# A two-layer hybrid model kernel: four buffers for modulation weights, small inputs packed, and output projections opened on two column slabs at once

## What is computed

```python
c_act = jax.nn.silu(c)
for layer in range(DEPTH):                         # DEPTH = 2
    mod = c_act @ ada_w[layer] + ada_b[layer]      # 1024 -> 6144
    shift_m, scale_m, gate_m, shift_f, scale_f, gate_f = ...split(mod, 6)
    h = rmsnorm(x, norm_mix_g[layer]) * (1.0 + scale_m) + shift_m
    y = gdn_mixer(h, ...) if layer % 2 == 0 else mla_mixer(h, ...)
    x = x + gate_m * y
    h = rmsnorm(x, norm_ffn_g[layer]) * (1.0 + scale_f) + shift_f
    x = x + gate_f * swiglu(h, ffn_w_gate[layer], ffn_w_up[layer], ffn_w_down[layer])

def gdn_mixer(h, w_in, conv_w, a_log, dt_bias, norm_g, w_out):
    proj = h @ w_in                                # q, k, v, gate: 4 x 1024; a, b: 8 each
    qkv = silu(causal_depthwise_conv(qkv, conv_w)) # 4 taps
    beta, g = sigmoid(b_in), -exp(a_log) * softplus(a_in + dt_bias)
    o = chunk_gated_delta_rule(l2norm(q), l2norm(k), v, g, beta)   # per head, chunks of 64
    o = rmsnorm(o, norm_g) * silu(gate)
    return o @ w_out                               # 1024 x 1024
```

## Time and profile before

| | us |
|---|---|
| runs | 2572.89, 2578.45, 2578.01 |
| median | 2578.01 |
| the profiled execution | 2574.89 |
| its span in the profile | 2573.1 |

### The profile page before, as it was taken

One profiled execution on the slowest core, in us unless ns is written; L12 is line 12 of the kernel. 1 busy time (PEld: TensorE's weight loads), 2 busy tenths in 40 slices (PEclk: granted clock), 3 DMA queues, 4 the chain that ended last, 5 costly groups with the idle time before them and its releaser, 6 DMA issues.

```text
span 2573.1 us, 29814 instructions
## 1 busy us (share of the span) xinstructions
PE 2323.3 (90%) x12156; PEld 1831.7 (71%) x12156; DVE 1185.8 (46%) x1734; ACT 609.6 (24%) x1101; POOL 1204.3 (47%) x690
## 2 busy tenths in 40 slices
PE   4899998999999978889999997878898889989888
PEld 2677776778888755557888885556677767878766
DVE  5566666575454653225313136334452254554332
ACT  3243343131111232222202023332221121012112
POOL 1323222357777732115666665113446556656552
PEclk8999999899999989889999998889999999999989
DMA  6322222155555411002333332002223223323221
GB/s 212 98 86 67 80 76 65 57 165 172 189 164 191 136 64 35 25 25 77 104 98 94 96 93 80 25 25 67 72 73 92 81 82 107 97 83 98 83 82 58
DMA packets 361699, 236.23 MB, mean 92 GB/s; under 512 B 11126, under 2 KB 346204, under 8 KB 361436
## 3 DMA queue, kind: packets, MB, share of 16 engines
q1 hardware_dynamic: 360732, 230.40, 30.1%
q10 hardware_dynamic: 832, 3.93, 0.4%
HBM read 232.21 MB, written 2.10 MB: 91 GB/s over the span
## 4 chain that ended last, share of the span: by engine, by line
PE 82%; DVE 11%; ACT 3%; DMA 2%; issue 2%; POOL 1%; SPq 0%; DVEq 0%; ACTq 0%; POOLq 0%
PE bank L457 16%; PE bank L458 16%; PE bank L459 16%; PE bank L476 4%; PE bank L478 3%; PE bank L477 3%; PE bank L652 2%; PE bank L501 2%; DVE A L1774 2%; PE bank L971 1%; DMA WIDE<-in_ada_t 1%; PE bank L961 1%; DVE mx L1758 1%; PE bank L824 1%; PE bank L493 1%
## 5 line engine op out<-in xcount | busy, mean ns | idle before, releaser
L419 POOL TENSOR_SCALAR wH<-stage 128x1024 fp32r<-128x1024 f32 (+3 forms) x342 | 381.8, 1116 | 1312.7 <-PE bank L459 539.3
L421 POOL TENSOR_TENSOR wL<-stage,wH 128x1024 fp32r<-128x1024 f32 (+3 forms) x342 | 823.5, 2408 | 28.5
L457 PE MATMUL bank<-hH,wH 128*128 128x512 f32 x1108 | 439.9, 397 | 25.9 <-ACT A L1083 8.4
L458 PE MATMUL bank<-hL,wH 128*128 128x512 f32 x1108 | 435.8, 393 | 0.0
L459 PE MATMUL bank<-hH,wL 128*128 128x512 f32 x1108 | 435.3, 393 | 0.0
L457 PE MATMUL bank<-RA,wH 128*128 128x512 f32 (+1 forms) x900 | 327.5, 364 | 13.8 <-DVE A L1466 13.8
L458 PE MATMUL bank<-RA,wH 128*128 128x512 f32 (+1 forms) x900 | 325.8, 362 | 0.0
L459 PE MATMUL bank<-RA,wL 128*128 128x512 f32 (+1 forms) x900 | 325.8, 362 | 0.0
L457 PEld LDWEIGHTS bank<-hH,wH 128*128 128x128 f32 x1108 | 211.1, 191 | 76.1 <-issue 25.3
L459 PEld LDWEIGHTS bank<-hH,wL 128*128 128x128 f32 x1108 | 210.9, 190 | 44.6
L458 PEld LDWEIGHTS bank<-hL,wH 128*128 128x128 f32 x1108 | 211.2, 191 | 44.1 <-issue 0.7
(11 more groups left out here) (304 smaller groups left out, 3198.8 us busy)
## 6 DMA issues: line engine op xcount, KB each, us to landing
WIDE<-in_ada_t SPq DMA_DIRECT2D x48, 1024.0 KB, 5.9
stage<-in_ffn_w_gate SPq DMA_DIRECT2D x44, 512.0 KB, 3.8
stage<-in_ffn_w_up SPq DMA_DIRECT2D x44, 512.0 KB, 3.8
stage<-in_gdn_w_in SPq DMA_DIRECT2D x32, 512.0 KB, 4.1
stage<-in_ffn_w_down SPq DMA_DIRECT2D x32, 512.0 KB, 4.0
stage<-in_c_wkv SPq DMA_DIRECT2D x32, 512.0 KB, 3.8
stage<-in_o_w_in SPq DMA_DIRECT2D x32, 512.0 KB, 4.0
stage<-in_e_w_in SPq DMA_DIRECT2D x26, 512.0 KB, 3.8
```

Of the source, the lines that this page charges most:

```text
L419: pool.tensor_scalar(high[:, 0:n], raw[:, 0:n], 1.0, 0.0, ALU.mult, ALU.add).then_inc(w_high, 1)
L421: pool.tensor_tensor(low[:, 0:n], raw[:, 0:n], high[:, 0:n].bitcast(F32), ALU.subtract).then_inc(w_split, 1)
L457: pe.matmul(bank[:, 0:n], h[:, k, c], xh[:, k, :], start=first and k == 0, stop=False)
L458: pe.matmul(bank[:, 0:n], h[:, k, c], xl[:, k, :], start=False, stop=False)
```

## The change

**Start.** The first eight modulation groups use four slots (two of them in `A`), and a load waits for the sum four groups earlier. The small inputs are packed on the host: gate columns (`gdn_ab`, 128 x 128), three vectors of eight, the convolution rows behind the tables. SP's order is new: c first, group 0 ahead of x, and slabs 0 to 2 between groups 5, 6 and 7. The gate columns have weights of their own (`abH`, `abL`) and no place in the slab plan. PE makes gate columns, slab 0 and slab 1 together, chunk by chunk, as h comes. DVE's and ACT's work on the gates is moved between head 0's convolutions. The first five chunks of head 1 are done before head 0's squares and not at its start.

**Openings.** All 12 calls of `residual` run slabs 0 and 1 in step: chunk n of slab 0, chunk n of slab 1, chunk n+1 of slab 0.

**Last head.** Its fills now issue 14 chunk products (seven chunks of two slabs) of `gdn_out`, so that only chunk 7 is left for `residual`.

```diff
-PLAN = [("ab", 2), ("gdn", 32), ("gdn_out", 8)]
+PLAN = [("gdn", 32), ("gdn_out", 8)]
+ADA_SLOT = [n % 4 if n < ADA_HEAD else n % 2 for n in range(2 * ADA_LAYER)]
...
+        adaw = [t.rearrange(...) for t in (WIDE[:, 0:4], WIDE[:, 4:8], A[:, 8:12], A[:, 12:16])]
+        abH, abL = RA[:, 16, 0:2 * P], RA[:, 17, 0:2 * P]
...
             def load_ada(n):
-                if n >= 2:
-                    sp.wait_ge(ada_summed, n - 1)
+                if n >= 4:
+                    sp.wait_ge(ada_summed, n - 3 if n < ADA_HEAD else n - 1)
...
-            head_slabs(0)
+            for n in range(2, ADA_HEAD):
+                load_ada(n)
+                if n >= ADA_HEAD - 3:
+                    j = n - ADA_HEAD + 3
+                    load(SLAB0["gdn"] + j, vin[8 * j], KD)
+            load(SLAB0["gdn"] + 3, vin[24], KD)
...
+            def residual_chunk(name, xh, xl, kc, n, k, j):
+                s0, u0 = SLAB0[name], USE0[name]
+                if n == 0:
+                    pe.wait_ge(w_split, s0 + j + 1)
+                    free(j, u0 // 2)
+                h, l = (w[:, k, :] for w in halves(s0 + j, kc))
+                pe.matmul(acc[j][:], h, xh[:, k, :], start=n == 0, stop=False)
+                pe.matmul(acc[j][:], h, xl[:, k, :], start=False, stop=False)
+                mm = pe.matmul(acc[j][:], l, xh[:, k, :], start=False, stop=n == kc - 1)
+                if n == kc - 1:
+                    mm.then_inc(slab_done, 1)
...
+                for n in range(begun, kc):
+                    pe.wait_ge(ready, count - kc + n + 1)
                     for j in range(2):
+                        residual_chunk(name, xh, xl, kc, n, order[n] if order else n, j)
+                if behind:
+                    behind(0)
+                for i in range(2, KD):
+                    slab(s0 + i, i % 2, u0 // 2 + i // 2, xh, xl, kc)
...
-                def fill(*chunks):
+                def fill(first, end):
                     if ahead:
-                        head_sums(i + 1, range(*chunks))
+                        head_sums(i + 1, range(first, end))
+                    else:
+                        for c in range(14 * first // 32, 14 * end // 32):
+                            pe.wait_ge(y_ready, c // 2 + 1)
+                            residual_chunk("gdn_out", yH, yL, KD, c // 2, c // 2, c % 2)
-                fill(0, 5)
+                if i:
+                    fill(0, 5)
...
-            residual("gdn_out", yH, yL, KD, y_ready, 8, 1)
+            residual("gdn_out", yH, yL, KD, y_ready, 8, 1, begun=KD - 1)
```

More of the change, by code:

```diff
@@ L111 @@
     _s += _n
-    _u += {"ab": 0, "mla": 24}.get(_name, _n)
+    _u += 24 if _name == "mla" else _n
 NORM_OF = {"mix0": 0, "ffn0": 1, "mix1": 2, "ffn1": 3, "e": 4, "x0": 5, "o": 6, "x1": 7}
@@ L126 @@
 ADA_FFN = 20
+ADA_SLOT = [n % 4 if n < ADA_HEAD else n % 2 for n in range(2 * ADA_LAYER)]
+ADA_NTH = [ADA_SLOT[:n + 1].count(ADA_SLOT[n]) for n in range(2 * ADA_LAYER)]
 ADA_EDGE = [ADA_FFN + j * (2 * ADA_LAYER - ADA_FFN) // FK for j in range(FK + 1)]
@@ L601, in _ @@
                 mm = pe.matmul(B3[:], l, hH[:, k, :], start=False, stop=k == KD - 1)
-            mm.then_inc(slab_done, 2)
+                if k == KD - 1:
+                    mm.then_inc(ab_done, 1)
+                for j in range(2):
+                    h, l = (w[:, k, :] for w in halves(SLAB0["gdn"] + j))
+                    pe.matmul(acc[j][:], h, hH[:, k, :], start=k == 0, stop=False)
+                    pe.matmul(acc[j][:], h, hL[:, k, :], start=False, stop=False)
+                    mm = pe.matmul(acc[j][:], l, hH[:, k, :], start=False, stop=k == KD - 1)
+                    if k == KD - 1:
+                        mm.then_inc(slab_done, 1)
             def gates_of_tokens():
@@ L1680, in head @@
                 if ahead:
-                    head_start(i + 1)
-            for j in range(3):
-                conv(0, j, (2, 1, 0))
-            head_start(0)
+                    head_decay(i + 1)
+                    head_scaled(i + 1)
+            ab = B3[:, 0:64].rearrange("p (t h) -> p t h", h=16)
+            dve.wait_ge(ab_done, 1)
+            dve.tensor_copy(A[0:16, 12], B3[0:16, :]).then_inc(g["abT"], 1)
+            conv(0, 0, (2, 1, 0))
+            dve.wait_ge(par_in, 16)
+            dve.wait_ge(g["ab"], 1)
+            own(dve.tensor_tensor(tmp8[:, 1], ab[:, :, 0:8], bc8[:, 1, :].unsqueeze(1).broadcast_to((P, TT, 8)), ALU.add))
+            own.settle()
+            own(dve.tensor_scalar(tmp8[:, 2], tmp8[:, 1], -1.0, None, ALU.mult))
+            own.settle()
+            dve.tensor_tensor(tmp8[:, 2], tmp8[:, 1], tmp8[:, 2], ALU.max).then_inc(g["azb"], 1)
+            conv(0, 1, (2, 1, 0))
+            dve.wait_ge(g["eb"], 1)
+            own(dve.tensor_scalar(tok[:, 1], tmp8[:, 0], 1.0, None, ALU.add))
+            own.settle()
+            own(dve.reciprocal(tok[:, 1], tok[:, 1]))
+            dve.wait_ge(g["sp"], 1)
+            own(dve.scalar_tensor_tensor(out=tmp8[:, 1], in0=tmp8[:, 1], scalar=0.0, in1=tmp8[:, 3], op0=ALU.max, op1=ALU.add))
+            own.settle()
+            dve.scalar_tensor_tensor(out=tok[:, 4], in0=tmp8[:, 1], scalar=-1.0,
+                                     in1=bc8[:, 0, :].unsqueeze(1).broadcast_to((P, TT, 8)),
+                                     op0=ALU.mult, op1=ALU.mult).then_inc(g["gates"], 1)
+            conv(0, 2, (2, 1, 0))
+            dve.wait_ge(g["gexp"], 1)
+            own(dve.tensor_copy(tok[:, 0], B4[:, 0:32].rearrange("p (t h) -> p t h", h=8)))
+            own.settle()
+            dve.tensor_tensor(tok[:, 3], B4[:, 32:64].rearrange("p (t h) -> p t h", h=8), tok[:, 0], ALU.subtract)\
+               .then_inc(g["zab"], 2)
+            dve.wait_ge(g["gexp"], 2)
+            own(dve.tensor_tensor(tok[:, 2], tok[:, 1], tmp8[:, 0], ALU.mult))
+            own.settle()
+            head_decay(0)
+            head_scaled(0)
             for i in range(0, 7):
```

173 lines of the change are left out of this document (68 added, 105 removed).

## The result

The changed kernel is slower: a median of 2591.25 us over seven executions (2581.36 to 2595.43) against 2572.89 for the kernel before (seven, 2566.74 to 2578.45), ratio 1.006 with a 95% interval of 1.0037 to 1.0083, or 9.5 to 21 us. The profiled execution took 2582.76 us, span 2580.9 at a mean granted clock of 0.957, the second fastest of the seven; it is 7.8 us longer than the profiled execution of before (2573.1, at a clock of 0.952).

What follows compares the result with a forecast made beforehand. TensorE, holding 82% of the chain, was taken as the bound, with VectorE and GpSimd taking turns. +1.8 − 1.8 + 1.5 − 0.6 + 10.3 = +11.2 on the median 2578.01 gave 2589.2 us, range 2574 to 2598.

Steps and rivals of the forecast that it cites:

- Start to norm: Start up to the norm: VectorE's modulation sums take turns with GpSimd's splits, TensorE starts at 50.6, +1.8 us.
- First product to head 0: From TensorE's first product to head 0's at 99.6: 49.0 us and not 50.8, −1.8, with a 6 us wait for gates.
- Last head: Last head: starts 9.7 us late behind splits of slabs 0 and 1, part comes back, in effect −0.6 us.
- The rival in which it waits for no split: Last head: no wait for GpSimd's splits, −6 instead of −0.6 us, time 2584; chance 0.12.
- (a): Ten openings: slab 2 waits for the first accumulator, which VectorE empties late, 0.43 us each, 4.3 in all.
- (b): Opening of `x1_out`: the output turn behind the pair needs slab 0 emptied and scaled, 1.3 us.
- (c): Six feed-forward openings: slab 1's first product waits for the second accumulator, 0.35 us each, 2.1 in all.
- (d): First feed-forward opening: slab 1 is split late, another 1.4 us.
- (e): Last `down` part: VectorE's chain starts 3.5 us later, makes up some, +2.0 us, replacing (a) and (c) there, so +1.2.
- Turns cost nothing: Rival for start, stretch to head 0 and last head: GpSimd's splits fall into VectorE's pauses, 2570 to 2573 us; chance 0.17.
- openings cost nothing: Rival for the openings: TensorE loads weights ahead, so no loss there, −10.3 us, time 2579; chance 0.12.
- Lower clock: Rival: the lower clock in head 0 and the last head, +5 us, time 2594; chance 0.15.

Runs made afterwards that it cites:

- the openings alone: All twelve residuals opened by two slabs in step, put into the kernel before without the other parts of the change: ratio 1.0086 (1.0066 to 1.0106).
- the order with the gates first: The new start alone, but VectorE forms all gates before any convolution, with gate sums ahead of v sums on TensorE: ratio 1.0021 (1.0008 to 1.0034).

## Why the prediction was right, and where its terms were off

The sign and the 2589.2 us came out (2591.25). By its steps:

- **Start to norm**, +1.8 foretold, first product 50.6: 50.09, +1.2. The mechanism, GpSimd's splits between the last modulation sums, was shown by holding one split back (46.80).
- **First product to head 0**, first product of head 0 at 99.6: 98.03. Gates late and a wait for them, yes: 4.5 us, not 6. The term for the lower clock, +1.5, was paid a few microseconds further on: −1.7 at head 0 became 0.0 at head 1. Start and stretch together are 0.0 where the terms made +1.5 (+1.8 − 1.8 + 1.5): 1.5 us too dear.
- **Last head**, first product 446.1: 446.15, behind waits of 4.75 and 1.82 us, 6.6 together, where the sign named was 8 to 10. The step at 454.5: 453.85. In effect −0.6: −1.3. The rival in which it waits for no split is out. That most of the 9.7 us comes back was right for the reason given: with TensorE waiting, VectorE meets one split and not three.
- **Openings**, +10.3: 14.9 at the next stage's first product, without the lag that `gdn_out` has (15.7 at the last product of each residual). The waits exist as described and go when slab 0 leads by two. Piece by piece: (a) 0.43 each was too small, 0.5 to 0.65 in the plain ones (0.3 at `o_out`, most of which came with openings apart too), since the product behind a wait also takes 0.31 and not 0.23 until the next; (b) 1.3, measured 1.3; (c) 0.35 each (its rows, 0.96 less 0.68, give 0.28), measured 0.55; (d) 1.4, measured 1.3; (e) is **the failed step**: a late start of 3.5 us was to be partly made up, 2.0 in all; nothing was made up, the chain even took 1.3 us longer, and the next stage starts 4.9 us later for it. The rows for this were in the trace of before: VectorE waits only some 0.8 us between most of the steps.
- **Turns cost nothing** and **openings cost nothing**: out, by the rows of the start (2.18 for the gain, 7.24 for three taps) and by the ratio of the openings alone.
- **Lower clock**, +5: not in the profiled execution, which gained 1 to 3 us between stages. The forecast's sum was +11.2; edits account for 0.0 − 1.3 + 14.9 = +13.6. Changes between the stages, where no edit lies, took 5.8 us off in this execution (1.2 behind `gdn_out`, 2.5 before `mla_out`, 0.8 behind the last `down` part, 0.7 and 0.6 after), which gives the 7.8 of the spans; in the first two the mean clock rose from 0.96 to 0.98 and from 0.85 to 0.87. The measured ratio, +15 us (9.5 to 21), agrees with the edits' sum.

That the number was so close is in part luck: a start and a last head dearer by 2 us than they were, an opening term 5 us too cheap, and above all the base. The forecast added its +11.2 to a median of 2578.01 from three executions; the seven measured beside the changed kernel have 2572.89. Against that base the medians differ by 18.4 us, 7 more than forecast, and the ratio says 15.

## What to carry to other kernels

Two accumulators run in step are meant to hide a late input. No run here shows them hiding one: eleven openings didn't wait for their input, and at `gdn_out`, where the last input arrives behind the first products (482.45 against 477.36), the step alone still cost 0.5 us. They make the reader of both start late and their next user wait. A lead of two chunks takes the waits away, not the late start, so ask first whether the stage behind is bound by the reader's chain.

Work put in to fill a wait must itself be ready at that point of the in-order queue: the same 14 chunks, begun where their slab is split, gave 7.3 us of lead and not 2.0. And moving one engine's step forward only helped here once the order on the next engine was moved with it (the v sums on ScalarE).

## What the runs showed of the hardware

- The kernel before spread over 15 to 20 us in its larger sets of executions, and most of it goes with the mean granted clock: over 35 executions of the kernel before, span and clock correlate at −0.92, about 2 us for each 0.001. Stage marks shift between two executions by up to 8 us where no edit lies (+8.4 before `mla_out` and −8.5 before `x1_out` with the openings in step, at clocks of 0.83 and 0.98 in these stretches, 0.85 and 0.92 before). Only the growth of the lag across the short stretch that holds the edit is safe to read.
- Tiny instructions grow most, against their own length, beside GpSimd. In the order with the gates first, on VectorE:

```profile
69.23 1.97 DVE L1686 TENSOR_SCALAR tmp<-tmp 128x32 f32<-128x32 f32 x1
71.23 0.98 DVE L1688 TENSOR_TENSOR tmp<-tmp 128x32 f32<-128x32 f32 x1
72.48 2.22 DVE L1691 TENSOR_SCALAR tok<-tmp 128x32 f32<-128x32 f32 x1 [0.27 <-ACT tmp L1206]
```

against 0.17 for a TENSOR_SCALAR of this shape and 0.19 for a TENSOR_TENSOR where nothing stood in the way (at 81.74 and 77.29 in the changed kernel). The first and the third have one input in the buffer. By the rule of the Trainium skill, "SBUF — State Buffer", section "SBUF: two separate sides", an instruction with two inputs there, or in a two-port mode, meets the lock; the trace agrees for those with two inputs and shows the same wait for this form with one, and whether that ran in such a mode no row tells.
